# Neighbourhood attention: scores from halves stacked in the rows, and the queries' norm as a scale per query

## What is computed

```python
q   = _heads(hx, w[:, :hd],       na_q_g)   # projected, then _rms over each head
k   = _heads(hx, w[:, hd:2 * hd], na_k_g)   # the same, for the tokens
k_c = _heads(hc, w[:, hd:2 * hd], na_k_g)   # ... and for the context
s_loc = einsum(q_r, k_win) * scale + bias   # scale = 64 ** -0.5
s_ctx = einsum(q_r, k_ctx) * scale
p = softmax(concatenate([s_loc, s_ctx]))
o = p_loc @ v_win + p_ctx @ v_ctx
```

## Time and profile before

| | us |
|---|---|
| median of 3 runs | 1315.74 (1315.54 to 1316.16) |
| span of the profiled execution | 1313.5 |
| median less span, that is what lies around it | 2.2 |
| PE busy | 1293.7 (98% of the span) |
| DVE busy | 871.0 (66%) |
| ACT busy | 596.3 (45%) |
| POOL busy | 428.0 (33%) |
| `na_in`, from chunk 2 to the last attention product | about 931 to 1113 on the trace's clock |

### The profile page before, as it was taken

One profiled execution on the slowest core, in us unless ns is written; L12 is line 12 of the kernel. 1 busy time (PEld: TensorE's weight loads), 2 busy tenths in 40 slices (PEclk: granted clock), 3 DMA queues, 4 the chain that ended last, 5 costly groups with the idle time before them and its releaser, 6 DMA issues.

```text
span 1313.5 us, 19893 instructions
## 1 busy us (share of the span) xinstructions
PE 1293.7 (98%) x7772; PEld 1103.8 (84%) x7772; DVE 871.0 (66%) x1303; ACT 596.3 (45%) x956; POOL 428.0 (33%) x433
## 2 busy tenths in 40 slices
PE   9999999999999999999999999999999999999999
PEld 8887999999887888788788888787777777999987
DVE  6597588999976587798433443334677665855553
ACT  6235656666654223253311233222555554766432
POOL 1373232333320002265300244011467552488200
PEclk9999999999999999999999999999999999999999
DMA  8776456555556344554444444345522321555552
GB/s 306 244 264 237 172 185 223 185 180 187 202 186 212 141 148 141 182 187 160 148 141 146 147 146 146 126 146 180 197 73 104 113 81 52 202 181 184 187 192 80
DMA packets 64476, 220.50 MB, mean 168 GB/s; under 512 B 7072, under 2 KB 10400, under 8 KB 64384
## 3 DMA queue, kind: packets, MB, share of 16 engines
q1 hardware_dynamic: 64096, 218.98, 47.8%
q10 hardware_dynamic: 288, 0.25, 0.1%
HBM read 217.73 MB, written 1.05 MB: 167 GB/s over the span
## 4 chain that ended last, share of the span: by engine, by line
PE 78%; DVE 12%; issue 4%; ACT 2%; DMA 1%; POOL 1%; SPq 0%; DVEq 0%; ACTq 0%; POOLq 0%
PE ps L616 19%; PE ps L630 18%; PE ps L628 18%; PE ps L606 7%; PE ps L608 4%; DVE wlo L1703 4%; DVE tmp L1988 2%; PE ps L1066 1%; DVE Y L1730 1%; PE ps L1093 1%; DMA raw<-in_w_in 1%; PE ps L1080 1%; PE ps L731 1%; PE ps L1059 1%; DVE A L2177 1%
## 5 line engine op out<-in xcount | busy, mean ns | idle before, releaser
L616 PE MATMUL ps<-A,whi 128*128 128x256 f32 (+2 forms) x1572 | 514.7, 327 | 0.0
L630 PE MATMUL ps<-A,wlo 128*128 128x256 f32 (+2 forms) x1544 | 494.0, 320 | 3.2 <-DVE wlo L1703 3.2
L628 PE MATMUL ps<-A,whi 128*128 128x256 f32 (+2 forms) x1544 | 493.4, 320 | 0.2 <-DVE A L1716 0.2
L1703 DVE TENSOR_TENSOR wlo<-raw,whi 128x1024 fp32r<-128x1024 f32 x303 | 395.3, 1308 | 84.9 <-ACT whi L1223 84.6
L1223 ACT ACTIVATE whi<-raw 128x1024 fp32r<-128x1024 f32 x303 | 317.7, 1051 | 263.9 <-PE ps L630 137.6
L616 PEld LDWEIGHTS ps<-A,whi 128*128 128x128 f32 x1572 | 298.9, 190 | 42.4 <-issue 18.5
L630 PEld LDWEIGHTS ps<-A,wlo 128*128 128x128 f32 x1544 | 293.4, 190 | 25.3 <-DVE wlo L1703 4.2
L628 PEld LDWEIGHTS ps<-A,whi 128*128 128x128 f32 x1544 | 294.0, 190 | 22.1 <-issue 1.7
L2379 POOL TENSOR_TENSOR H<-tmp,H 128x256 fp32r<-128x256 f32 (+1 forms) x86 | 125.6, 1461 | 56.2 <-ACT H L1538 42.7
L606 PE MATMUL ps<-H,whi 128*128 128x512 f32 x400 | 140.2, 395 | 0.2 <-POOL H L2379 0.2
L608 PE MATMUL ps<-H,wlo 128*128 128x256 f32 x400 | 112.3, 281 | 0.6 <-DVE wlo L1703 0.6
(11 more groups left out here) (320 smaller groups left out, 1495.1 us busy)
## 6 DMA issues: line engine op xcount, KB each, us to landing
raw<-in_ada SPq DMA_DIRECT2D x96, 512.0 KB, 4.3
raw<-in_w SPq DMA_DIRECT2D x64, 512.0 KB, 3.4
raw<-in_w_up SPq DMA_DIRECT2D x44, 512.0 KB, 4.3
raw<-in_w_in SPq DMA_DIRECT2D x36, 512.0 KB, 5.9
raw<-in_w_0a SPq DMA_DIRECT2D x32, 512.0 KB, 3.6
raw<-in_w_0b SPq DMA_DIRECT2D x32, 512.0 KB, 3.5
raw<-in_na_in SPq DMA_DIRECT2D x24, 512.0 KB, 5.4
raw<-in_w_down SPq DMA_DIRECT2D x22, 512.0 KB, 4.2
```

The costliest lines, as they stand in the source:

```text
L616: e.matmul(o, w_hi, ah, start=k == 0, stop=False)
L628: e.matmul(o, w_hi, al, start=False, stop=False)
L630: m = e.matmul(o, w_lo, ah, start=False, stop=last)
L1703: e.tensor_tensor(wlo[i % NRAW][:, :cols], raw[i % NRAW][:, :cols], plain(whi[s % NHI][:, :cols]), SUB).then_inc(S("wlo").sem, 1)
```

## The change

Three things are changed, all in `na_in`.

**Scores.** The queries of a head are written as high half (fp32r) into the head's own 64 rows, and as low half (value less high half) into the other head's 64 rows of the same columns, so that one tile of 128 rows holds both halves of one head. The keys' high half is written twice, to both sets of 64 rows (`k_hi`); the keys' low half stands in the head's own rows, over zeros in the other 64 (`k_lo`). One product of 128 rows with `k_hi` then gives (high + low of the queries) by high of the keys, a second with `k_lo` adds high by low. A score bank is now filled by two fp32r products of 128 rows instead of one float32 matmul of 64 rows. ACT writes `k_hi` in four copies of 64x512 per pair (`keys_hi`), DVE `k_lo` in two subtractions (`keys_lo`) and the queries' low half in two subtractions of 64x256 that read the chunk's own bank (`queries_lo`), which is a new condition for that bank's next use (`q_lo`).

**Norm of the queries.** They are no longer multiplied. Their squares now stand as weights of two small float32 matmuls with two moving columns each, so that the sums come out with queries in the partitions, 128x4 for a pair. Mean, root and Newton step work on 128x4, the Newton step on DVE instead of POOL (`query_newton`), with the 0.125 in its constants. The result is the scale that DVE applies when it reads the scores, in place of the constant. The keys are multiplied by both gains.

**Start.** Four tiles of 64x512 are set to zero, and the two gains are multiplied, on DVE between the last low halves of the normed activations and the first unit of `na_in`.

```diff
         def head_sum(j, src, T, n):
             w.wait_ge(S("na"), n + 1)
-            o = turn_bank("norm", j)[:, :T]
-            e.matmul(o, const("blocks"), src, start=True, stop=True).then_inc(S("hn_sum").sem, 1)
+            o = turn_bank("norm", j)
+            if j % 2 == 0:
+                e.matmul(o[:, :T], const("blocks"), src, start=True, stop=True).then_inc(S("hn_sum").sem, 1)
+                return
+            for b in range(2):
+                m = e.matmul(o[:, 2 * b:2 * b + 2], src[:, 128 * b:128 * b + 128], const("blocks")[:, 0:128:64],
+                             start=True, stop=True)
+            m.then_inc(S("hn_sum").sem, 1)
...
-            w.wait_ge(S("hn_out"), 2 * p + 2)
+            w.wait_ge(S("k_lo"), 2 * p + 2)
+            w.wait_ge(S("q_lo"), 2 * p + 2)
+            w.wait_ge(S("key_zero"), 4)
             for x in range(2):
                 o = turn_bank("scores", 4 * p + 2 * b + x)
-                e.matmul(o, q2[p % 3][rows_of(x), 128 * b:128 * b + 128], k2[p % 3][rows_of(x), :],
-                         start=True, stop=True).then_inc(S("s2_mm").sem, 1)
+                query = q2[p % 3][:, 256 * x + 128 * b:256 * x + 128 * b + 128]
+                e.matmul(o, query, k_hi[p % 2][x], start=True, stop=False)
+                e.matmul(o, query, k_lo[p % 2][x], start=False, stop=True).then_inc(S("s2_mm").sem, 1)
...
+        def keys_hi(c):
+
+            w.wait_ge(S("hn_out"), c + 1)
+            if c >= 2:
+                w.wait_ge(S("s2_mm"), 4 * (c - 2) + 4)
+            for x in range(2):
+                for at in range(2):
+                    e.activation(k_hi[c % 2][x][rows_of(at)], k2[c % 2][rows_of(x)], ACT.Copy).then_inc(S("k_hi").sem, 1)
...
+        def queries_lo(c, n):
+
+            o, into = bank_of("na_in", n), q2[c % 3]
+            w.wait_ge(S("q_hi"), 2 * c + 2)
+            w.wait_ge(S("na"), n + 1)
+            for x in range(2):
+                e.tensor_tensor(into[rows_of(1 - x), half(x)], o[rows_of(x), :256], plain(into[rows_of(x), half(x)]),
+                                SUB).then_inc(S("q_lo").sem, 1)
...
+        def keys_lo(c):
+
+            w.wait_ge(S("k_hi"), 4 * c + 4)
+            for x in range(2):
+                e.tensor_tensor(k_lo[c % 2][x][rows_of(x)], k2[c % 2][rows_of(x)], plain(k_hi[c % 2][x][rows_of(x)]),
+                                SUB).then_inc(S("k_lo").sem, 1)
...
         def during_na(n):

+            if n and NA_CHUNKS[n - 1][0] == "q":
+                queries_lo(NA_CHUNKS[n - 1][1], n - 1)
             if norm2(n - 2):
-                j, dst, T = norm2(n - 2)
-                head_out(j, T, dst, param("q_g" if j % 2 else "k_g"))
+                j, dst, _ = norm2(n - 2)
+                query_newton(j // 2) if j % 2 else key_out(j // 2, dst)
             if norm2(n - 1):
                 j, _, T = norm2(n - 1)
                 head_mean(j, T)
             written("na_in", n)
+            if n >= 3 and NA_CHUNKS[n - 3][0] == "k":
+                keys_lo(NA_CHUNKS[n - 3][1])
```

81 lines of the change are left out of this document (58 added, 23 removed).

## The result

| | before | after the change |
|---|---|---|
| median of 10 runs each, us | 1315.53 (1313.72 to 1316.16) | 1316.87 (1316.21 to 1319.40) |
| profiled execution: time / span, us | span 1313.5 | 1319.17 / 1317.4 |
| stage, us | 197.89 | 201.49 |

A forecast was written before the change was run, and what follows sets the result against it. PE, busy 98% of the span, was taken as the bound. Terms -5.4 + 1.3 + 0 + 0.25 + 0.6 = -3.25 us gave a span of 1310.25 and a median of 1312.5 us; range 1309.0 to 1315.8.

The forecast's parts named there:

- The score products: PE's score calls: four fp32r products at 0.23 us replace float32 matmuls, saving 0.34 us in each of 16, 5.4 us.
- the query sums: PE's sums of the queries' squares: 0.60 us instead of 0.43, a loss of 0.17 in each of 8, 1.3 us.
- rival of slow products: Stacked score products on PE run at 0.31 us, not 0.23; the 5.4 us are gone: +2.15, 1317.9; chance 0.02.
- The late calls: Six score calls whose second matmul waits for DVE's mean: lateness of 5.1 us unchanged, 0; bounds -3 to +2 us.
- The keys' halves: ACT's copies and DVE's subtractions per pair: PE loses 0.25 us once, between scores (1, 0) and (1, 1).
- The zeros: Four memsets and a small product on DVE at the stage's start: 0.6 us lost, bounds 0 and 1.0.
- The sum of k1's squares: At the first pair, squares come near 945.9 and PE wants them at 946.01: cover 0.1 us, nothing charged.
- The vector queue takes most of it: Keys' subtractions take 1.08 instead of 0.6 us through POOL contention; 0.25 us more lost in 8 pairs: -1.25, 1314.5; chance 0.27.
- A chain of their own: DVE waits for ACT's copies with score reading queued behind; 8 rounds hold PE about 1.1 us each: +5.55, 1321.3; chance 0.09.
- signs of error: Wrong if PE waits for banks at other calls too, or DVE's wait for ACT's copies exceeds 0.5 us a round.

The follow-up runs named there:

- the kernel without low halves: Changed kernel with queries' mean first, zeros by POOL, constant scale, and both kinds of low halves left out: stage 190.27 us, ratio 0.9937 to the kernel before.
- second profile: The changed kernel run and profiled once more, nothing altered: stage 200.93 us, median 1317.99 us, ratio 1.0022 to the kernel before.
- all three cures: Changed kernel with zeros by POOL, queries' mean first, and keys' low halves behind the reading of the scores: stage 198.22 us, ratio 0.9998 to the kernel before.
- ACT's copies later: Kernel with all three cures, plus ACT's copies of the keys' high halves moved behind the chunk's squares: stage 202.61 us, ratio 1.0030 to the kernel before.
- lean: Changed kernel, all means first, zeros and queries' Newton step by POOL, keys' low halves behind the reading of scores: stage 199.42 us, ratio 0.9999 to before.
- zeros by POOL: Changed kernel with the four tiles of zeros written by POOL instead of DVE: stage 200.26 us, ratio 1.0013 to the kernel before.
- constant scale: Changed kernel with DVE reading the scores with constant 0.125 instead of the scale per query: stage 198.92 us, ratio 1.0000 to the kernel before.
- mean first: Changed kernel with DVE's mean of a query chunk ahead of queries' low halves and keys' multiplication: stage 199.62 us, ratio 1.0002 to the kernel before.
- zeros and mean: Changed kernel with zeros by POOL and the queries' mean first, keys' low halves left in place: stage 198.98 us, ratio 1.0009 to the kernel before.

## Why the prediction was wrong

**The score products (-5.4) and the query sums (+1.3): the sum of the two was right, by two errors that cancel.** A call behind turning is 0.32 us shorter (0.34 forecast). But I took this price for all 16 calls, and only 9 stand behind turning. The three behind products with values gain less: from the start of (1, 1) to the sum of k3's squares it was 2.60 us before and 2.47 in the kernel without low halves, and 2.60 and 2.46 from (3, 1) to k5. The query sums went the other way. PE's timeline of q2's:

```profile
970.80 0.51 PE L1075 MATMUL ps<-con,sq 128*128 128x2 f32 x4
971.17 0.47 PE L626 MATMUL ps<-A,whi 128*128 128x512 f32 x1
971.48 0.39 PE L638 MATMUL ps<-A,whi 128*128 128x512 f32 x1
```

From 970.80 to 971.48, less 0.23 for the product in it, is 0.45 us, where it was 0.43 and I had 0.60. The kernel without low halves shows 3.6 us of gain with 1.75 us still waited; against that stand the 1.2 us of lateness that are left in the kernel it is compared with. That makes about 4.2 (an estimate), where the two terms said 4.1. The rival of slow products is out.

**The late calls (0): mis-sized, and their cause not seen.** PE's idle time at them is 5.9 us in six calls. Measured as I measured before, by how much a call exceeds an undelayed one (0.9 to 1.05 us now), the lateness is 7.5 us in the first profile and 8.0 in the second, against 5.1: a loss of 2.4 to 2.9, beyond the bound of 2. And I took the 5.1 us as given. The earlier trace rows showed their cause, and mended alone it was 4.0 us; a mean that frees a bank stood behind a multiplication that nobody waited for.

**The keys' halves (+0.25) failed; this is the step.** The prices were fair: 1.40 us for two subtractions (1.2 to 2.0 forecast), 2.58 for four copies (2.0), 0.88 for the queries' two (0.7), and DVE's busy time grew by 18.2 us in 187, where I had 18. What failed was "at the other places ... the wait is a few tenths in idle time". Between the same events of before and of the second profile of after, the stage grew by 1.0 ahead of each of the sums of k3 and k5 and by 0.4 at q2's sum: 2.4 us where 0.25 stood, and at sums that the late calls don't touch. By another 0.4 to 0.5 it grew from (1, 0) and (3, 0) to the next call, and by 0.2 from (0, 1), (2, 1) and (4, 1) to the next sum, where the late calls have their share. "One place" was three to eight. Taking out the keys' low halves brought 3.4 us (3.0 without the start), and they cost 3.6 with all three cures.

I compared the added work with idle time summed over a round, and called the idle time cover. In sum it was there. DVE's idle time for PE in the window, in front of readings, of copies of turned probabilities and of copies of products (L2264, L2278, L2286), was 29.1 us and is 7.2; about as much went into the 18.2 us of added work and the new wait of 4.8 for ACT's copies. But it lay unevenly. In the dense chunks, 945 to 1040, DVE waited 8.1 us before reciprocals for ACT and 5.2 for POOL's Newton steps, and in the changed kernel these are still 7.1 and 5.3: work placed in front of such a wait leaves it nearly as it was. Only the 11.5 us in which DVE waited for PE were cover there, and of those 0.1 is left.

**The reading of the scores was left out of the sum.** I gave the scale no price. 0.06 us each lengthened a call's reading by 0.25; the constant put back was worth 2.0 us. The earlier start that I counted on (0.46 us after a call begins) was less early, too: the reading of (0, 0), whose call starts at 951.86, begins at 952.58, 0.72 later.

**The zeros (+0.6): right at 0.7**, with memsets at 0.65 us from start to start (0.6 forecast). Here the Trainium skill ("VectorE: DVE Perf Modes", Zero memsets can be issued as uint32) is worth a line. Its one cycle per element gave an estimate of 0.53 us each; the rows show 0.48 busy but 0.65 apart. Over all 128 rows, in the kernel without the keys' low halves, they are 0.48 busy and 0.54 apart, close to the page's estimate.

**The sum of k1's squares** was "a row to watch". It waited 0.42 us for ACT (0.46 in the second profile), and from the sum of q0's squares to it the stage grew by 0.6 us. ACT's copies took 2.58 us instead of 2.0, each starting 0.66 after the last, where I had 0.48. That row is a copy out of PSUM, though, and these read SBUF. But the length isn't the whole cause: with the mean of the queries first, and copies as long as before, the growth was 0.02 us. The mean of q0 stood behind the keys' multiplication, which waits for POOL, and ACT waits for this mean before it goes on to the copies.

**The rivals.** "The vector queue takes most of it" had the mechanism, but put it down to contention with POOL at 1.08 us per subtraction. The subtractions took 0.69, and in the changed kernel no contention shows in them; the rule of the Trainium skill on two inputs in SBUF ("SBUF — State Buffer", Who interferes with whom) is borne out only weakly (0.85 to 0.95 us where they were moved, in the kernels with all three and with ACT's copies later). That they were slower for POOL's sake there isn't shown. The amount of work and where it stood did it. "A chain of their own" had the other half: DVE waits up to 0.74 us for ACT's copies with the reading behind it, but it held PE by 1.0 us at two places and not by 1.1 at eight. The time lies between the two, at the edge of what I called slower. I gave them 0.27 and 0.09. My own signs of error both came true: PE waits at other calls (k3, k5), and DVE's wait for the copies, 0.74 us above, exceeds 0.5.

## What to carry to other kernels

Before a change hands work to a second engine, walk that engine's queue in order and ask of every instruction that frees a bank what stands ahead of it; the cheapest gain here was a three-line move in the kernel as it stood, and it was visible in the rows that the prediction used. Busy share is not slack: with DVE at 66%, 18 us of added work cost PE some 7 us (about 4 saved in its own work, 3.0 lost in the end), because idle time that is spent waiting in order for a slower engine covers little of what is placed before the wait. Mend the queue's order first, and then price the change against the mended kernel: against that, this change loses 7.0 us of stage as it is and 4.3 with all three cures.

## What the runs showed of the hardware

- A DVE instruction of 128x256 that reads PSUM took 0.476 us with its factor in a column of SBUF, 0.413 to 0.418 with a constant.
- Four DVE memsets of 64x512 float32 were busy for 0.48 us each and started 0.65 apart; of 128x512 they were busy for 0.48 and started 0.54 apart (no low halves of keys).
- Copies on ACT of 64 rows by 512 out of SBUF took 0.63 us and started 0.66 apart; of 128 rows by 512 out of PSUM they took 0.59 and the next instruction started 0.48 to 0.50 later. Logarithms of 128 rows by 512 out of SBUF took 0.63 too: half the rows were not cheaper.
- A subtraction of 64x512 took 0.69 us on DVE (0.85 to 0.95 in the kernels with all three and with ACT's copies later), 1.43 on POOL.
- Behind waits of PE of 1.3 to 2.2 us the granted clock of a window of 5 us was 0.66 (changed), 0.67 (lean, zeros by POOL), 0.69 (constant scale), 0.75 (mean first) or 0.82 (zeros and mean) of the 2.4 GHz level, and 1.00 in other profiles with waits as long. While it was at the 1.2 GHz level, products came 0.43 us apart.
